# A mixture-of-experts kernel: gathering token rows straight into feature-major tiles

## The chip, the cores and the metric

The kernel runs on one core of a Trainium2 chip. The metric is the device time of one execution in microseconds, as the median of the runs of a kernel.

## The reference, cut to what matters

A decoder trunk of two layers (a gated convolution, then a retention layer), each with cross-attention and a mixture of experts. 288 tokens go through it: 256 of a prompt and 32 of eight short samples. Everything is float32. The part that the change touches is the mixture:

```python
def one_seq(hs):                       # hs: tokens x 1024
    ...                                # top group of 4, then the two best of its 8 experts
    gate = jnp.sum(jax.nn.one_hot(eidx, N_EXPERTS) * wts[..., None], axis=1)
    gu = jnp.einsum('td,edf->tef', hs, w_gate_up)          # 32 experts, 1024 -> 2 x 256
    act = jax.nn.silu(gu[..., :EXPERT_FF]) * gu[..., EXPERT_FF:] * gate[..., None]
    return jnp.einsum('tef,efd->td', act, w_down)          # 256 -> 1024
```

Only two of 32 experts have a nonzero gate for a token, so the kernel computes each expert only for the tokens that chose it.

## The kernel before, in words

The 32 experts of a layer are worked off in 8 **packs** of 4 (`PK`); each expert has 32 slots (`CAP`), so a pack has 128 slots, one per partition. For tokens beyond the slots of an expert there is a second pass (`spill`), a loop whose count is read at run time.

Per pack and layer, `experts(L)` on TensorE does in this order:

- four **gate-up chunks** (`gate_up_chunk`, L905): chunk c multiplies feature tiles 2c and 2c + 1 of `xgT` (features on partitions, slots as columns) by 2 MB of weights; four experts side by side in column tiles of 32. Each waits for its weights to land and its end (`gu_sum`) frees their slot.
- in pack 0 `count_chosen`; then the **gather** `pick(i + 1)` for the next pack. It multiplies a 0/1 matrix `onehot` (tokens x slots, made by `select` on VectorE) with the token rows: `picked_decode` (L872) is four float32 matmuls of 32 rows each for the 32 sample tokens, each on its own quarter of the array's rows, and `picked_prompt(m)` (L879) two full matmuls for the prompt tokens, for each of four blocks of 256 features. The result has slots on partitions, in banks 0, 1, 5 and 6.
- in packs 0, 1, 3 and 5 of layer 0 a projection of the memory for layer 1 (`memory_kv`, L618 and L624), with 2 MB of weights that occupy a slot of the ring;
- the transposes of the gates (L937) and, once ScalarE and VectorE have made them, of the activations (L942); the result of the pack before is spread over the tokens and added (`combine`, L953);
- `turn_x(i + 1)` (L966): ScalarE and VectorE have copied the gathered rows out of the banks to `xg` (`picked_out`, L1539 and L1944); eight transposes (`turn_picked`, L947) turn them, and each engine copies one half to `xgT` (`turned_out`);
- two halves of the down projection (`down_half`, L921); their end (`y_sum`) frees the two slots.

In front of pack 0 stand `pick(0)` and `turn_x(0)`, with nothing in between. A float32 matmul shows in the trace as two instructions, each with its own weight load.

On VectorE (L1958 on) the order is `select(0)`, `gates_known`, `gates(0)`, `picked_out(0)`, `turned_out(0)`, `select(1)`, `passes_known`, and then the packs.

SyncE issues all loads of weights in one fixed order (`RING`). The ring has 7 slots of 2 MB (some loads go to free memory beside it), and each issue waits until the slot's last user is done: in layer 0 the load after that of `dn (0,1,0)` waits for the first memory projection of pack 0, those after it for the two halves of the down projection of pack 0.

Of the kernel before, what the change touches and what calls it, by code (L numbers as in the profile page):

```python
# [23 lines left out]
P = 128  # L24
# [21 lines left out]
SPILL_PE = {"picked": 1, "turned": 2, "gate_up": 3, "gates_turned": 4, "act_turned": 5, "rows": 6}  # L46
SPILL_DVE = {"began": 1, "selected": 2, "gated": 3, "x_out": 7, "xt_out": 9, "gates_out": 10, "silu": 11, "act": 12,
             "actT_out": 13, "rows_out": 15, "added": 23}
STEP_PE, STEP_DVE = 14, 22
# [78 lines left out]
def build(nc, a):  # L128

    with ExitStack() as ctx:  # L130
# [122 lines left out]
        XGO = CATO + 2048 + SLOT  # L253
# [3 lines left out]
        yo, xg = ar(CATO, 1024), ar(CATO + 1024, 1024)  # L257
# [8 lines left out]
        xgT_x, xg_x = v3(ar(HM1, 1024), KD), ar(HM1 + 1024, 1024)  # L266


# [314 lines left out]
        def _(pe):  # L583
# [288 lines left out]
            def picked_decode():  # L872

                for m in range(4):
                    r = slice(32 * m, 32 * m + 32)
                    pe.matmul(bank[X_BANKS[m]][:, 0:256], onehot_m[r, 2, :], htok3[r, :], start=True, stop=False,
                              skip_group_check=True)

            def picked_prompt(m):  # L879

                for b in range(2):
                    mm = pe.matmul(bank[X_BANKS[m]][:, 0:256], onehot_m[:, b, :], htok[b][:, m * 256:(m + 1) * 256],  # L882
                                   start=False, stop=(b == 1), skip_group_check=True)
                return mm
# [60 lines left out]
            def turn_picked(n, src):  # L945
                for k in range(4):
                    mm = pe.transpose(bank[n][:, k * P:(k + 1) * P], src[:, (4 * n + k) * P:(4 * n + k + 1) * P],  # L947
                                      C("ident"))
                return mm

# [4 lines left out]
            def experts(L):  # L955

                def pick(i):
# [45 lines left out]
                pick(0)  # L1003
                turn_x(0)
                for i in range(PACKS):
# [3 lines left out]
                    pe.wait_ge(S("xt_out_a"), PACKS * L + i + 1)  # L1009
                    if i >= 2:  # L1010
                        pe.wait_ge(S("y_added"), KD * PACKS * L + KD * (i - 1))
                    for c in range(4):
                        if c == 2:
                            pe.wait_ge(S("xt_out_d"), PACKS * L + i + 1)
                        if c == 2 and i == PACKS - 1:
                            combine(i - 1, range(0, 5))
                        if c == 3 and i == PACKS - 1:
                            combine(i - 1, range(5, KD))
                        gate_up_chunk(c, gate_up_landed(L, i, c), xgT).then_inc(S("gu_sum"), 1)
                    if i == 0:  # L1020
                        count_chosen()
# [22 lines left out]
                    if i + 1 < PACKS:  # L1044
                        turn_x(i + 1)
# [9 lines left out]
                with pe.If(more > 0):  # L1055
                    pe.wait_ge(S("y_added"), KD * PACKS * L + KD * PACKS)
                    with pe.Fori(0, more) as p:
                        with pe.Fori(0, PACKS) as i:
                            it = p * PACKS + i
                            pe.wait_ge(S(f"spill_dve{L}"), it * STEP_DVE + SPILL_DVE["selected"])  # L1060
                            picked_decode()
                            for m in range(4):
                                mm = picked_prompt(m)
                            mm.then_inc(S(f"spill_pe{L}"), 1)
                            pe.wait_ge(S(f"spill_dve{L}"), it * STEP_DVE + SPILL_DVE["x_out"])
                            turn_picked(0, xg_x)
                            turn_picked(1, xg_x).then_inc(S(f"spill_pe{L}"), 1)
# [1518 lines left out]
```

## Time and profile before

| | |
|---|---|
| three runs | 1156.84, 1157.18, 1157.6 us (median 1157.18) |
| profiled execution: span from first to last instruction | 1157.5 us |
| what lies around the span | not shown apart from the runs' times: the median lies 0.3 us below the span |
| mean granted TensorE clock | 0.98 of full |
| TensorE busy | 1100.7 us, 95% |
| VectorE, ScalarE, GpSimd busy | 510.1, 172.3, 154.0 us |
| read from HBM, written | 339.3, 24.3 MB |

The span starts with layer 0's projections; its experts run from about 287 us to 514 us, the retention layer's mixing from there to 943 us, its experts from 944 us to 1146 us, and the final norm ends the kernel. "Busy" is time in which an engine executes; PE is TensorE's matmuls, PEld its weight loads, which run beside the matmuls. "PEclk" is the share of the full clock (2.4 GHz) that was granted. In the chain of waits each piece is work, or a wait for the engine or transfer that is named, followed back from the last instruction. A DMA piece begins when the slot that it fills was released. The chain's duration of a group is without the overlap with the next; the timeline's includes it, so it is 0.1 to 0.2 us longer.

### The profile page before, as it was taken

To read this page: it belongs to the slowest core of one execution; us is meant where nothing else is said; L and a number is where in the kernel's file an instruction comes from. 1 tells how busy PE (TensorE), PEld (TensorE's weight loads), DVE (VectorE), ACT (ScalarE), POOL (GpSimd) and SP (SyncE) were. 2 spreads that over 40 slices of the span, in tenths; PEclk is the share of its full clock that TensorE was granted. 3 is DMA by queue.
4 is the path that set the end of the run, shared out by engine and by line. 5 is a ranking of instruction groups with operands and counts; after the bars stand their busy time and mean duration, and the time that the engine had idled before them with its cause. 6 is when DMAs were issued, how large, how long until landed. Compare 5 with 4: busy or idle time off the path is not lost.

```text
span 1157.5 us, 17239 instructions
## 1 busy us (share of the span) xinstructions
PE 1100.7 (95%) x7334; PEld 750.3 (65%) x7334; DVE 510.1 (44%) x1089; ACT 172.3 (15%) x410; POOL 154.0 (13%) x103
## 2 busy tenths in 40 slices
PE   8999999999999999979999999999999999987885
PEld 6589997987574545435767657576699755433342
DVE  5446665633213232345444545545465333322234
ACT  2001113013101111020201112020200131100002
POOL 0000001510000000002432324340055100000000
PEclk9999999998999999989999999999999989999998
DMA  9973339835999999969436656487997369999993
GB/s 362 429 273 146 147 146 392 344 146 219 369 429 424 427 426 427 426 270 399 192 154 255 272 208 256 186 332 291 409 422 304 144 270 430 424 427 429 426 427 149
DMA packets 29904, 364.81 MB, mean 315 GB/s; under 512 B 3472, under 2 KB 3616, under 8 KB 7296
## 3 DMA queue, kind: packets, MB, share of 16 engines
q1 hardware_dynamic: 26928, 339.86, 71.4%
q10 hardware_dynamic: 1712, 19.17, 4.0%
q0 software_dynamic: 1184, 4.63, 1.0%
q8 instruction: 61, 1.00, 0.3%
q14 instruction: 19, 0.16, 0.0%
HBM read 339.32 MB, written 24.32 MB: 314 GB/s over the span
## 4 chain that ended last, share of the span: by engine, by line
PE 85%; DMA 13%; DVE 1%; issue 1%; ACT 0%; SPq 0%; DVEq 0%
DMA ring<-in_gu 10%; PE bank L1198 10%; PE bank L725 10%; PE bank L1134 9%; PE bank L910 7%; PE bank L1272 5%; PE bank L624 5%; PE bank L618 4%; PE bank L921 4%; PE bank L882 4%; PE bank L953 3%; DMA ring<-in_dn 3%; PE bank L766 3%; PE bank L1107 3%; PE bank L1191 2%; PE bank L683 1%
## 5 line engine op out<-in xcount | busy, mean ns | idle before, releaser
L910 PE MATMUL bank<-ring,arena 128*32 128x512 f32 x888 | 107.5, 619 | 27.3 <-DMA ring<-in_gu 27.3
L725 PE MATMUL bank<-arena,ring 128*128 128x144 f32 x896 | 110.4, 286 | 1.3 <-issue 1.3
L725 PEld LDWEIGHTS bank<-arena,ring 128*128 128x128 f32 x896 | 110.0, 190 | 1.5 <-issue 1.5
L910 PEld LDWEIGHTS bank<-ring,arena 128*32 128x32 f32 x888 | 28.0, 112 | 97.0 <-issue 67.8
L1933 DVE TENSOR_TENSOR xT<-xT,bank 128x288 f32<-128x288 f32 x128 | 58.2, 455 | 39.2 <-PE bank L953 35.6
L953 PE MATMUL bank<-arena 128*128 128x288 f32 x256 | 70.2, 417 | 3.2 <-issue 2.8
L953 PEld LDWEIGHTS bank<-arena 128*128 128x128 f32 x256 | 46.5, 192 | 27.3 <-issue 11.2
L1198 PEld LDWEIGHTS bank<-ring 128*128 128x128 f32 x448 | 56.2, 190 | 6.0 <-issue 6.0
L882 PE MATMUL bank<-arena 128*128 128x256 f32 x256 | 60.0, 388 | 0.0
L2400 POOL TENSOR_TENSOR ring<-ring 128x1024 f32<-128x1024 f32 x8 | 18.9, 2359 | 307.1 <-DVE arena L2260 307.1
L1198 PE MATMUL bank<-ring 128*128 128x144 f32 x448 | 58.2, 287 | 0.0
L1272 PE MATMUL bank<-ring,hT 128*128 128x512 f32 x128 | 57.2, 597 | 0.0
L921 PE MATMUL bank<-ring,arena 128*32 128x512 f32 x448 | 54.3, 623 | 1.7 <-DMA ring<-in_dn 1.2
L624 PE MATMUL bank<-ring,arena 128*128 128x512 f32 x128 | 55.4, 592 | 0.0
L1927 DVE SCALAR_TENSOR_TENSOR arena<-arena,bank 128x256 f32<-128x256 f32 x16 | 6.7, 419 | 110.4 <-ACT arena L1556 110.4
L882 PEld LDWEIGHTS bank<-arena 128*128 128x128 f32 x256 | 47.7, 191 | 11.5 <-issue 5.6
L2065 DVE SCALAR_TENSOR_TENSOR ring<-ring,bank 128x512 f32<-128x512 f32 x64 | 39.7, 683 | 32.9 <-PE bank L1191 32.9
L618 PE MATMUL bank<-arena,ring 128*128 128x256 f32 x224 | 51.6, 392 | 0.0
L1198 PEld LDWEIGHTS bank<-hT,ring 128*128 128x128 f32 x384 | 48.3, 190 | 2.7 <-issue 2.7
L1198 PE MATMUL bank<-hT,ring 128*128 128x144 f32 x384 | 49.8, 286 | 0.0
L618 PEld LDWEIGHTS bank<-arena,ring 128*128 128x128 f32 x224 | 44.0, 197 | 6.7 <-issue 0.4
L1272 PEld LDWEIGHTS bank<-ring,hT 128*128 128x128 f32 x128 | 23.6, 190 | 30.5 <-issue 30.4
(329 smaller groups left out, 1589.6 us busy)
## 6 DMA issues: line engine op xcount, KB each, us to landing
ring<-in_gu SPq DMA_DIRECT2D x55, 2048.0 KB, 21.6
ring<-in_dn SPq DMA_DIRECT2D x28, 2048.0 KB, 20.2
ring<-in_rin SPq DMA_DIRECT2D x14, 2048.0 KB, 13.4
ring<-in_cin SPq DMA_DIRECT2D x8, 2048.0 KB, 27.3
ring<-in_kc SPq DMA_DIRECT2D x8, 2048.0 KB, 10.1
ring<-in_vc SPq DMA_DIRECT2D x8, 2048.0 KB, 9.5
ring<-in_st SPq DMA_DIRECT2D x8, 2048.0 KB, 8.2
out_rs<-ring ACTq DMA_DIRECT2D x8, 2048.0 KB, 7.1
```

Source lines behind the costliest of these rows:

```text
L618: mm = pe.matmul(bank[KV_BANKS[i][j]][:, o * NM:(o + 1) * NM], w[:, k, f:f + P], src[:, k, :], start=(k == 0), stop=(k == KD - 1), skip_gr ...
L624: mm = pe.matmul(bank[KV_BANKS[i][j]][:, :], src[:, k, mb * P:(mb + 1) * P], w[:, k, :], start=(k == 0), stop=(k == KD - 1))
L725: mm = pe.matmul(out[:, o, :], w[:, o, k, :], x[:, k, :], start=(first and o == 0 and k == 0), stop=(k == 3), skip_group_check=True)
L882: mm = pe.matmul(bank[X_BANKS[m]][:, 0:256], onehot_m[:, b, :], htok[b][:, m * 256:(m + 1) * 256], start=False, stop=(b == 1), skip_group_ ...
L910: mm = pe.matmul(bank[2][32 * e:32 * e + 32, :], xt[:, k, 32 * e:32 * e + 32], w[2 * e + kk], start=(k == 0), stop=(k == KD - 1), skip_gro ...
L921: mm = pe.matmul(out if n == 0 else v3(out, 2), actT[:, f, 32 * e:32 * e + 32], wv[2 * e + f] if n == 0 else wv[:, 2 * e + f], start=(f == ...
L953: return pe.matmul(bank[b][:, 0:T], yo[:, o * P:(o + 1) * P], GT, start=True, stop=True)
L1134: mm = pe.matmul(out[:, o, :], w[:, o, k, :], x[:, k, :], start=(first and o == 0 and k == 0), stop=(k == 3), skip_group_check=True)
L1198: mm = pe.matmul(out[:, o, :], w[o][:, k, :], x[:, k, :], start=(first and o == 0 and k == 0), stop=(k == 3), skip_group_check=True)
L1272: mm = pe.matmul(bank[4 + b][:, :], hT[:, k, b * P:(b + 1) * P], w[:, k, :], start=(k == 0), stop=(k == KD - 1))
L1933: return dve.tensor_tensor(xT[:, o, :], xT[:, o, :], bank[b][:, 0:T], ALU.add)
L2065: dve.scalar_tensor_tensor(out=st[:, j, dt, :], in0=st[:, j, dt, :], scalar=float(np.exp(NS * LOGG[h])), in1=quad_banks(h)[j][:, :], op0=A ...
```

## The change

The gather's operands change places. The token rows (128 features of them) become the stationary operand and `onehot` the moving one, so that the bank holds features on partitions and slots as columns, which is what `xgT` needs. For each of the 8 feature tiles there is one matmul of 32 rows for the sample tokens and two full ones for the prompt tokens, all with 128 columns. `xg`, `turn_picked`, `turn_x` and `turned_out` go; the copies out of the banks write `xgT` directly. In pack 0 the gather of feature tiles 0 to 3 stands in front, tiles 4 and 5 are gathered after gate-up chunk 0, tiles 6 and 7 after chunk 1. On VectorE `picked_out(0)` moves in front of `gates_known` and `gates(0)`. The loop for the second pass is changed in the same way and left out here.

```diff
-            def picked_decode():
-
-                for m in range(4):
+            def picked(m):
+
+                for k in (2 * m, 2 * m + 1):
+                    out = bank[X_BANKS[m]][:, (k % 2) * P:(k % 2 + 1) * P]
                     r = slice(32 * m, 32 * m + 32)
-                    pe.matmul(bank[X_BANKS[m]][:, 0:256], onehot_m[r, 2, :], htok3[r, :], start=True, stop=False,
+                    pe.matmul(out, htok3[r, (k % 2) * P:(k % 2 + 1) * P], onehot_m[r, 2, :], start=True, stop=False,
                               skip_group_check=True)
-
-            def picked_prompt(m):
-
-                for b in range(2):
-                    mm = pe.matmul(bank[X_BANKS[m]][:, 0:256], onehot_m[:, b, :], htok[b][:, m * 256:(m + 1) * 256],
-                                   start=False, stop=(b == 1), skip_group_check=True)
+                    for b in range(2):
+                        mm = pe.matmul(out, htok[b][:, k * P:(k + 1) * P], onehot_m[:, b, :], start=False,
+                                       stop=(b == 1), skip_group_check=True)
                 return mm
...
-                def pick(i):
+                def pick(i, pairs=range(4)):
                     pe.wait_ge(S("selected"), PACKS * L + i + 1)
...
-                    picked_decode()
-                    for m in range(4):
-                        picked_prompt(m).then_inc(S("x_picked"), 1)
-
-                def turn_x(i):
-                    for n in range(2):
-                        pe.wait_ge(S("xg_out_a"), 2 * PACKS * L + 2 * i + n + 1)
-                        pe.wait_ge(S("xg_out_d"), 2 * PACKS * L + 2 * i + n + 1)
-                        turn_picked(n, xg).then_inc(S("xg_turned"), 1)
+                    for m in pairs:
+                        picked(m).then_inc(S("x_picked"), 1)
...
-                pick(0)
-                turn_x(0)
+                pick(0, (0, 1))
                 for i in range(PACKS):
...
-                    pe.wait_ge(S("xt_out_a"), PACKS * L + i + 1)
...
                     for c in range(4):
-                        if c == 2:
-                            pe.wait_ge(S("xt_out_d"), PACKS * L + i + 1)
+                        pe.wait_ge(S("xt_out_d" if c % 2 else "xt_out_a"), 2 * PACKS * L + 2 * i + c // 2 + 1)
                         if c == 2 and i == PACKS - 1:
+                            pe.wait_ge(S("xt_out_d"), 2 * PACKS * L + 2 * i + 2)
                             combine(i - 1, range(0, 5))
...
                         gate_up_chunk(c, gate_up_landed(L, i, c), xgT).then_inc(S("gu_sum"), 1)
+                        if i == 0 and c < 2:
+                            pick(0, (c + 2,))
...
                     if i + 1 < PACKS:
-                        turn_x(i + 1)
+                        pe.wait_ge(S("xt_out_a"), 2 * PACKS * L + 2 * i + 4)
+                        pe.wait_ge(S("xt_out_d"), 2 * PACKS * L + 2 * i + 4)
                     pe.wait_ge(S("actT_out"), PACKS * L + i + 1)
...
                 def picked_out(i):
                     for m in (0, 2):
                         act.wait_ge(S("x_picked"), 4 * PACKS * L + 4 * i + m + 1)
-                        act.activation(xg[:, m * 256:(m + 1) * 256], bank[X_BANKS[m]][:, 0:256], ACT.Copy) \
-                           .then_inc(S("xg_out_a"), 1)
...
+                        act.activation(xgT[:, 2 * m:2 * m + 2, :], picked_bank(m), ACT.Copy) \
+                           .then_inc(S("xt_out_a"), 1)
...
                 select(0)
+                maxima_known(L)
+                picked_out(0)
                 gates_known(L)
                 gates(0)
-                picked_out(0)
-                turned_out(0)
                 dve.wait_ge(S("gated"), PACKS * L + 1)
                 select(1)
```

`maxima_known` is the first part of the old `gates_known` (two small instructions), split off so that ScalarE's exponentials don't wait for the copies. VectorE's `picked_out` and the second pass change alike.

## Rows read from the trace of the kernel before

**Rows 1.** the page: TensorE's busy time, then transfers in 40 slices of the span.
```profile
PE 1100.7 (95%) x7334; PEld 750.3 (65%) x7334; DVE 510.1 (44%) x1089; ACT 172.3 (15%) x410; POOL 154.0 (13%) x103
...
DMA  9973339835999999969436656487997369999993
GB/s 362 429 273 146 147 146 392 344 146 219 369 429 424 427 426 427 426 270 399 192 154 255 272 208 256 186 332 291 409 422 304 144 270 430 424 427 429 426 427 149
```

**Rows 2.** chain that ended last, 285:345: start us, us, what.
```profile
286.83 0.64 PE bank L876 x8
287.47 3.67 PE bank L882 x16
...
291.73 0.63 PE bank L947 x4
292.36 7.00 PE bank L910 x64
...
312.09 0.87 PE bank L947 x8
...
327.69 13.83 PE bank L618 x64
```

**Rows 3.** TensorE's waits, 430:515: us in total, times, longest us.
```profile
PE bank L910 <- DMA ring<-in_gu: 5.8, 4, 2.0
```

**Rows 4.** stretches: us, busy PE to POOL (x instructions), PEclk, DMA share, GB/s.
```profile
294.00:296.00 2.00, 2.00 (x24) 0.65 (x20) 0.00 (x0) 0.00 (x0) 0.00 (x0) 1.00 0.67 193
310.00:313.00 3.00, 3.00 (x24) 2.42 (x26) 0.42 (x1) 1.34 (x3) 0.00 (x0) 1.00 0.48 153
```

**Rows 5.** DMA issues in 311:311.7, 404.5:405, 965.9:966.6, 986.6:987: KB, us to landing.
```profile
ring<-in_dn SPq DMA_DIRECT2D x1, 2048.0 KB, 7.9
...
ring<-in_dn SPq DMA_DIRECT2D x1, 2048.0 KB, 9.0
...
ring<-in_gu SPq DMA_DIRECT2D x1, 2048.0 KB, 9.5
...
ring<-in_gu SPq DMA_DIRECT2D x1, 2048.0 KB, 13.4
```

**Rows 6.** whole chain that ended last: mid-layer rows, and layer 0's memory projection.
```profile
382.96 13.75 PE bank L624 x32
...
779.81 2.16 PE bank L1198 x16
781.97 1.07 PE bank L1191 x8
...
840.82 68.97 PE bank L725 x560
```

**Rows 7.** TensorE's timeline at 323.9:324.1, then line L882: min/median/max ns.
```profile
323.97 0.48 PE L882 MATMUL bank<-arena 128*128 128x256 f32 x1
...
L882 PE MATMUL bank<-arena x256: 379/379/796, 287.4 to 1104.4; 128*128 128x256 f32 x128
```

**Rows 8.** VectorE's timeline, 286.9:289.9: start us, us, line, operation.
```profile
286.93 0.18 DVE L1895 RECIPROCAL arena<-arena 128x3 f32<-128x3 f32 x1 [2.35 <-ACT arena L1534]
...
289.24 0.56 DVE L1922 TENSOR_TENSOR arena<-arena 128x384 f32<-128x384 f32 x1
```

**Rows 9.** half clock: one stretch, then rows of the chain in both layers.
```profile
498.00:506.00 8.00, 6.88 (x37) 1.77 (x37) 1.27 (x3) 0.80 (x2) 0.00 (x0) 0.57 1.00 426
...
498.07 2.70 PE bank L910 x16
...
503.34 3.18 PE bank L921 x16
...
509.48 1.85 PE bank L921 x16
...
1066.86 31.66 DMA ring<-in_gu
...
1134.08 3.54 PE bank L921 x16
```

More of the change, by code:

```diff
@@ L45 @@
 PACKS = NE // PK
[L46 to L49, printed above, removed]
+SPILL_PE = {"picked": 1, "gate_up": 2, "gates_turned": 3, "act_turned": 4, "rows": 5}
+SPILL_DVE = {"began": 1, "selected": 2, "gated": 3, "xt_out": 7, "gates_out": 8, "silu": 9, "act": 10,
+             "actT_out": 11, "rows_out": 13, "added": 21}
+STEP_PE, STEP_DVE = 13, 20
 FIRST = ((0, 2), (2, 4), (4, 8))
@@ L251, in build @@
         assert ro[0] <= PHO + ROUTE and PHO + ROUTE + 3072 <= 20992
-        XGO = CATO + 2048 + SLOT
+        XGO = CATO + 1024
         htok_ = v3(ar(PHO + ROUTE, 2048), 2)
@@ L256, in build @@
         htok3 = ar(PHO + ROUTE + 2048, 256)
-        yo, xg = ar(CATO, 1024), ar(CATO + 1024, 1024)
+        yo = ar(CATO, 1024)
         onehot = ar(SQO, 3 * P).rearrange("p (b c s) -> p b c s", b=3, c=PK)
@@ L264, in build, with picked_bank @@
         xgT = v3(ar(XGO, 1024), KD)
-        xgT_x, xg_x = v3(ar(HM1, 1024), KD), ar(HM1 + 1024, 1024)
+        xgT_x = v3(ar(HM1, 1024), KD)
+        def picked_bank(m):
+            return v3(bank[X_BANKS[m]][:, 0:256], 2)
         def slot(s):
@@ L943, in turn_act @@
                 return mm
[L945 to L949, printed above, removed]
             def spread(o, b):
@@ L1060, in experts @@
                             pe.wait_ge(S(f"spill_dve{L}"), it * STEP_DVE + SPILL_DVE["selected"])
-                            picked_decode()
                             for m in range(4):
-                                mm = picked_prompt(m)
+                                mm = picked(m)
                             mm.then_inc(S(f"spill_pe{L}"), 1)
-                            pe.wait_ge(S(f"spill_dve{L}"), it * STEP_DVE + SPILL_DVE["x_out"])
-                            turn_picked(0, xg_x)
-                            turn_picked(1, xg_x).then_inc(S(f"spill_pe{L}"), 1)
                             pe.wait_ge(S(f"spill_dve{L}"), it * STEP_DVE + SPILL_DVE["xt_out"])
@@ L1541, in picked_out @@
                         act.wait_ge(S("x_picked"), 4 * PACKS * L + 4 * i + m + 1)
-                        act.activation(xg[:, m * 256:(m + 1) * 256], bank[X_BANKS[m]][:, 0:256], ACT.Copy) \
-                           .then_inc(S("xg_out_a"), 1)
-                def turned_out(i):
-                    act.wait_ge(S("xg_turned"), 2 * PACKS * L + 2 * i + 1)
-                    act.activation(xgT[:, 0:4, :], v3(bank[0][:, :], 4), ACT.Copy).then_inc(S("xt_out_a"), 1)
+                        act.activation(xgT[:, 2 * m:2 * m + 2, :], picked_bank(m), ACT.Copy) \
+                           .then_inc(S("xt_out_a"), 1)
                 picked_out(0)
-                turned_out(0)
                 for i in range(PACKS):
@@ L1885, in route, with maxima_known @@
                                             op0=ALU.add, op1=ALU.mult))
-            def gates_known(i):
+            def maxima_known(i):
                 dve.wait_ge(S("rstd_tok"), i + 1)
@@ L1893, in gates_known @@
                    .then_inc(S("gate_maxima"), 1)
+            def gates_known(i):
                 dve.wait_ge(S("gate_exps"), 6 * i + 6)
@@ L1946, in picked_out @@
                         dve.wait_ge(S("x_picked"), 4 * PACKS * L + 4 * i + m + 1)
-                        dve.tensor_copy(xg[:, m * 256:(m + 1) * 256], bank[X_BANKS[m]][:, 0:256]).then_inc(S("xg_out_d"), 1)
-                def turned_out(i):
-                    dve.wait_ge(S("xg_turned"), 2 * PACKS * L + 2 * i + 2)
-                    dve.tensor_copy(xgT[:, 4:8, :], v3(bank[1][:, :], 4)).then_inc(S("xt_out_d"), 1)
+                        dve.tensor_copy(xgT[:, 2 * m:2 * m + 2, :], picked_bank(m)).then_inc(S("xt_out_d"), 1)
                 def add_pack(i, part=range(KD)):
@@ L1980, in experts @@
                     if i + 1 < PACKS:
-                        turned_out(i + 1)
                         dve.wait_ge(S("gt_turned"), PACKS * L + i + 1)
@@ L2015, in experts @@
                             for m in range(4):
-                                dve.tensor_copy(xg_x[:, m * 256:(m + 1) * 256], bank[X_BANKS[m]][:, 0:256]) \
-                                   .then_inc(S(f"spill_dve{L}"), 1)
-                            dve.wait_ge(S(f"spill_pe{L}"), it * STEP_PE + SPILL_PE["turned"])
-                            for n in range(2):
-                                dve.tensor_copy(xgT_x[:, 4 * n:4 * n + 4, :], v3(bank[n][:, :], 4)) \
+                                dve.tensor_copy(xgT_x[:, 2 * m:2 * m + 2, :], picked_bank(m)) \
                                    .then_inc(S(f"spill_dve{L}"), 1)
```

3 lines of the change are left out of this document (removed).

## The prediction

> **What bounds the kernel now.** I read the page first [rows 1]. TensorE is busy for 95% of the span, so time added to it has little slack to vanish in. The two stretches that the change touches are the experts of layer 0 (about 287 to 514 us) and of layer 1 (about 944 to 1146 us). There the transfers run at their full rate too, so each part of these stretches has to be asked which of the two ends last.
>
> The chain of waits for layer 0 [rows 2] shows TensorE pieces without a break through pack 0: gather, transposes, gate-up chunks, the projection of the memory, the transposes of gates and activations. TensorE's list of waits for that stretch has 5.8 us for gate-up weights, in four pieces, all after 430 us [rows 3]. Layer 0 is thus TensorE-bound for its first five packs and shared in the last three. In the page's DMA row the slices from 318 us to 492 us are full [rows 1]. Before that there are two pauses: 294 to 296 us at 193 GB/s and 310 to 313 us at 153 GB/s, against 427 in a full slice [rows 4]. Both end with the issue of a load for whose slot SyncE had to wait. The one of 311 us landed 7.9 us later, which is what a load takes that finds the queue empty; one that finds a queue lands later, at 4.9 us per load (2.10 MB at 427 GB/s) [rows 1, 5]. So a load issued at time t lands at t + 8 or 4.9 us after the one before, whichever is later. The loads issued at 405, 966 and 987 us landed 9.0, 9.5 and 13.4 us later [rows 5]: they had 1.0, 1.5 and 5.4 us to spare before the queue would have run dry. In layer 1 the queue never runs dry, and its last packs go at the pace of the transfers.
>
> **The gather, old and new.** Now one gather takes 0.64 + 3.67 = 4.31 us [rows 2]: 8 instructions of 32 rows (four at a time, side by side) and 16 of the full array (a float32 matmul is two instructions), with 256 columns each. It changes tiling twice, into the 32-row tiles and out of them. The new gather has for each of 8 feature tiles one 32-row matmul and two full ones, with 128 columns: 24 matmuls, 48 instructions. It changes tiling 16 times, and the four 32-row matmuls no longer run side by side.
>
> The bare pace: 560 instructions of 144 columns take 68.97 us, 0.123 us each, so 128 columns take 0.109 us, and transposes with 128 columns take 0.87 / 8 = 0.109 too [rows 2, 6]. 48 x 0.1095 = 5.26 us.
>
> A change of tiling, worked out twice. In the gather, 64 instructions of 256 columns take 13.83 us, 0.216 each; 16 of these and two rounds of the 32-row ones make 18 x 0.216 = 3.89, and 4.31 is 0.42 more, 0.21 per change [rows 2]. In the retention stage 16 full instructions of 144 columns alternate with 8 of 32 rows and 512 columns: 2.16 + 1.07 = 3.23 us, of which 16 x 0.123 + 2 x 0.43 = 2.83 is bare work; 0.40 for two changes, 0.20 each [rows 6]. The timeline shows where it goes: the first full matmul after the 32-row ones takes 0.48 instead of the usual 0.38 us (its weights are loaded in the open, 0.10), and the other 0.10 passes before that load starts [rows 7]. So 16 x 0.20 = 3.2 us, and **a new gather costs 8.46 us**, 4.15 more than the old. Bounds: 5.26 if a change in the middle of an accumulation were free, 9.3 at 0.25 per change. I take 0.20, because both places in the trace give it and the new alternation is of the same two tilings.
>
> **What else is on TensorE.** Removed: the eight transposes, 0.87 us in each of packs 0 to 6 [rows 2], and in front of pack 0 the wait for the row copies and the transposes, 291.14 to 292.36 us, 1.2 us [rows 2]. In pack 0 those 0.87 us also covered the copy of the turned activations on VectorE; without them TensorE waits for it, about 0.45. Added in pack 0: two more returns from the gather to a chunk, 0.4. The copies of rows (4 per pack) become copies into the final tile and the two of 0.6 to 0.7 us go; they hide behind the rest of the gather, so nothing is gained there. VectorE's order changes in pack 0: `gates_known` and `gates`, 286.93 to 289.80 us now, 2.9 us [rows 8], move behind the copy of the last pair, and `select(1)` behind them, for which the second gather waits. The last pair is gathered before chunks 2 and 3, and TensorE has those (3.5 us), a return and `count_chosen` (0.8) to do: 4.5 us against 0.4 + 2.9 + 0.6 = 3.9. It fits, with 0.6 to spare. No DMA issue moves by itself: SyncE's order is the same, and each issue follows TensorE's release of its slot.
>
> **Layer 0.** Eight gathers: 8 x 4.15 = 33.2. Plus 0.4 and 0.45, less 7 x 0.87 = 6.1 and 1.2: TensorE has 26.8 us more to do. Against it stand the waits for transfers, 5.8 [rows 3], which vanish when TensorE is the later one, and the half clock from 499 to 506 us (granted share 0.57 in 498 to 506, one of the two levels, 1.2 GHz) that follows those waits: 3.18 us for 16 instructions that take 1.85 at full clock, and 2.70 for a chunk that takes 7.00 / 4 = 1.75, together 2.3 us [rows 2, 9]. Layer 0 ends 26.8 - 5.8 - 2.3 = **18.7 us later**, if the transfers don't end later still. They: pack 0's early chunk closes the pause at 294 us, but the next load waits for the memory projection behind the second gather, which comes 4.15 + 0.4 - 1.2 + 4.15 = 7.5 us later, so the early slot is given back at once. The load now issued at 405 us follows gathers 0 to 4 and comes 16.9 us later; it has 1.0 to spare, so the transfers fall 16 us behind. TensorE, 26.8 us later before waits are taken off, stays the later one.
>
> **Layer 1.** Its packs go at the pace of the transfers, so only a pause in these counts. The issue at 966 us follows two gathers and the first half of pack 0's down projection: 4.15 + 0.4 - 1.2 + 4.15 - 0.87 + 0.45 = 7.1 us later, with 1.5 to spare: **5.5 us**. The one at 987 us comes 7.1 + 3.3 = 10.4 later with 5.4 to spare, 5.0: no more. From there the reserve is larger than what TensorE loses (3.3 us per pack): it grows with every pack, and by 1067 us a load lands 31.7 us after its slot is released [rows 9].
>
> **Sum.** 1157.5 (span) + 18.7 + 5.5 = 1181.7. The span is 0.3 us above the median of the three times shown, 1157.2; against that median the forecast is **1181 us**.
>
> **The rivals.** *Half of each change is hidden.* The weights of the next matmul are loaded during the last one of the other tiling, and only the 0.10 of emptying is left: gather 5.26 + 1.6 = 6.9 us. Then layer 0 has only 14 us more on TensorE, the transfers are the later ones (8.9 - 1.0 = 7.9), layer 1 loses 3.9 - 1.5 = 2.4: 1167. Against it: the open load in [rows 7]. The Trainium skill ("TensorE: Matmul & The Clock Gate", Step-by-step) says that weight loads are pulled ahead of matmuls in flight when row groups don't conflict or the background buffer is free, which would give this case; "TensorEngine Tiling (Array Packing)", Key Properties, says that a change of tiling mode drains the engine, and gives no price. The rows side with the second.
>
> *A change costs nothing inside an accumulation.* Gather 5.26 us; the issue at 311 us comes 1.1 later, layer 1 loses nothing: 1158, within 0.2%. For it: no row shows a change between two matmuls of one accumulation. Against: the engine, not the bank, changes.
>
> *The clock stays up, and the kernel is faster.* Place: the last packs of both layers, where TensorE idles for transfers and then works at half clock, 2.3 us lost in layer 0 and in layer 1 3.54 instead of 1.8 us for 16 instructions at 1134 us, 1.7 [rows 9]. A longer gather fills that idling. With a gather of 5.26 us this gives 1157.2 + 1.1 - 4.0 = 1154. It decides only if the gather stays under about 5.5 us: each further 0.1 us is paid twice before the load of 311 us, and five times before that of 405 us.
>
> *Dearer than thought.* At 0.25 per change each gather is 0.8 longer, 6.4 us in layer 0 and 1.6 in layer 1: 1189. A missed `selected` in pack 0 adds at most 1.
>
> **Chances.** Forecast (gather 8 to 9 us, 1176 to 1187) 0.78; half hidden 0.08; free 0.06; clock 0.04; dearer than 1189 0.04. The range runs from the half-hidden case to the dearer one, 1165 to 1189, and leaves out about 0.14. A measurement of this kernel can tell 0.2% (2.3 us) from no change: faster 0.04, same 0.05, slower 0.91.
>
> **What would show it.** In the profile after, the gather's line should have 48 instructions per pack in about 8.5 us of the chain, each first weight load after a change starting 0.2 us behind the matmul before. The waits for gate-up weights should be gone from layer 0 and smaller in layer 1, the granted clock full around 518 us, a longer pause of transfers before 319 us and a new one near 992 us. Gathers of 5 to 7 us would prove the forecast wrong, as would layer 0 ending less than 12 us later.

## The result, and the profile after

The changed kernel takes 1190.55 us (four runs: 1184.76, 1186.83, 1194.26, 1197.39) against 1157.39 for the kernel before on the same chip. The ratio is 1.0265, 95% interval 1.0237 to 1.0294: slower, as forecast, but the median lies 1.5 us above the upper end of the range and 9.5 above the forecast. A second set of four runs gave 1186.9 (1185.16 to 1192.14). Each run is 1.7 to 1.9 us longer than its span. The profiled execution is the longest of the first four: 1197.39 us, span 1195.6. One of the 12 runs of the last kernel below took 1409.51 us at a mean granted clock of 0.749 and is left out of the ratio.

The page of the kernel after, rows that answer to [rows 1], with the granted clock and the gather's two lines (L881 the 32 rows of the samples, L884 the prompt), columns as in the page:

```profile
PE 1160.1 (97%) x7590; PEld 796.1 (67%) x7590; DVE 499.1 (42%) x1073; ACT 163.2 (14%) x394; POOL 154.1 (13%) x103
...
PEclk9999999998999999999999999999999959999979
DMA  9964449728699899968436557469995296999992
GB/s 361 428 241 151 170 175 417 283 82 346 276 418 406 354 396 428 427 256 373 197 152 267 243 220 288 196 247 375 428 425 221 88 369 272 425 427 429 425 426 99
...
L884 PE MATMUL bank<-arena 128*128 128x128 f32 x512 | 98.2, 318 | 0.0
...
L881 PE MATMUL bank<-arena 32*128 32x128 f32 x256 | 66.5, 341 | 0.0
```

TensorE went up by 59 us of busy time, and the transfers have new or longer gaps: 276 and 354 GB/s in the slices from 299 and 389 us, and 272 in the one from 986 us, where the same slices of [rows 1] have 369, 427 and 430. The clock's row has a 5 and a 7 in the experts of layer 1 that the kernel before doesn't have.

The chain of waits of after, layer 0, pack 0 (answers to [rows 2]; start us, us, what):

```profile
286.23 0.41 PE bank L881 x2
286.64 0.64 PE bank L884 x4
...
290.45 1.85 PE bank L912 x16
292.30 0.41 PE bank L881 x2
292.71 0.64 PE bank L884 x4
...
302.84 0.30 PE bank L881 x2
303.14 0.64 PE bank L884 x4
...
311.17 6.91 PE bank L622 x32
...
318.88 0.44 DVE arena L1955
```

and its timeline there (start us, us with overlap, shapes):

```profile
303.07 0.71 PE L884 MATMUL bank<-arena 128*128 128x128 f32 x4
303.72 0.48 PE L881 MATMUL bank<-arena 32*128 32x128 f32 x2
304.13 0.71 PE L884 MATMUL bank<-arena 128*128 128x128 f32 x4
```

A feature tile is 0.41 + 0.64 = 1.05 us; the gather for pack 1 begins at 302.7 and the projection behind it at 311.17: 8.45 us. TensorE's waits from 430 to 520 us no longer have a row for gate-up weights (5.8 us before [rows 3]). The only one left is:

```profile
PE bank L944 <- ACT arena L1443: 0.3, 1, 0.3
```

The pause of transfers before the load that was issued at 311 us is longer (answers to [rows 4]; columns as there), and the load lands 8.1 us after its issue at 318.11 [rows 5]:

```profile
312.00:318.00 6.00, 6.00 (x30) 5.23 (x29) 0.00 (x0) 0.00 (x0) 0.00 (x0) 1.00 0.00 0
```

**Where the 38.1 us between the two spans are.** I measure each layer's expert stage from the first instruction of its gather to the end of its last `combine` matmul:

| us | layer 0 | between | layer 1 | span |
|---|---|---|---|---|
| before | 227.6 | 429.7 | 201.5 | 1157.5 |
| after, profiled | 245.9 | 431.5 | 220.0 | 1195.6 |
| after, second profile | 245.9 | 432.4 | 209.5 | 1185.0 |

Layer 0 costs 18.3 us and does so to the hundredth in both profiles; the stretch between, which the change doesn't touch, 1.8 and 2.7; layer 1 costs 18.6 in one and 8.1 in the other. (The start of layer 0 came 0.6 and 1.5 us earlier; with that the sums close.) So layer 1 holds both the error of the forecast and the spread of the runs.

### The profile page after: what moved, and what is told of

The parts are those of the page before. It is cut to its first block, busy times and chain, and to the rows that moved or that the text cites. A ratio compares the mean times of both kernels' runs of the same rounds, so it can differ in the third digit from the quotient of the medians.

```text
span 1195.6 us, 17731 instructions
## 1 busy us (share of the span) xinstructions
PE 1160.1 (97%) x7590; PEld 796.1 (67%) x7590; DVE 499.1 (42%) x1073; ACT 163.2 (14%) x394; POOL 154.1 (13%) x103
## 4 chain that ended last, share of the span: by engine, by line
PE 95%; DMA 3%; DVE 1%; issue 1%; ACT 0%; SPq 0%; DVEq 0%
PE bank L1184 9%; PE bank L729 9%; PE bank L1120 9%; PE bank L912 9%; PE bank L884 7%; PE bank L949 5%; PE bank L1258 5%; PE bank L628 5%; PE bank L881 5%; PE bank L923 4%; PE bank L622 4%; PE bank L1093 3%; PE bank L770 3%; DMA ring<-in_gu 2%; PE bank L1177 1%; PE bank L687 1%
## 5 line engine op out<-in xcount | busy, mean ns | idle before, releaser
L912 PE MATMUL bank<-ring,arena 128*32 128x512 f32 x888 | 106.2, 615 | 5.3 <-DMA ring<-in_gu 5.1
L729 PEld LDWEIGHTS bank<-arena,ring 128*128 128x128 f32 x896 | 110.0, 190 | 1.8 <-issue 1.7
L884 PE MATMUL bank<-arena 128*128 128x128 f32 x512 | 98.2, 318 | 0.0
L884 PEld LDWEIGHTS bank<-arena 128*128 128x128 f32 x512 | 72.4, 204 | 17.0 <-issue 3.4
L1915 DVE TENSOR_TENSOR xT<-xT,bank 128x288 f32<-128x288 f32 x128 | 58.2, 454 | 28.4 <-PE bank L949 24.8
L1929 DVE COPY arena<-bank 128x256 f32<-128x256 f32 x32 | 13.6, 425 | 134.6 <-PE bank L884 134.6
L881 PE MATMUL bank<-arena 32*128 32x128 f32 x256 | 66.5, 341 | 0.0
L949 PEld LDWEIGHTS bank<-arena 128*128 128x128 f32 x256 | 46.7, 192 | 25.3 <-issue 9.2
L881 PEld LDWEIGHTS bank<-arena 32*128 32x128 f32 x256 | 40.5, 197 | 31.9 <-issue 20.2
L923 PE MATMUL bank<-ring,arena 128*32 128x512 f32 x448 | 51.4, 595 | 2.5 <-DVE arena L1955 2.5
## 6 DMA issues: line engine op xcount, KB each, us to landing
ring<-in_cin SPq DMA_DIRECT2D x8, 2048.0 KB, 28.4
```

Of the source, the lines that this page charges most:

```text
L729: mm = pe.matmul(out[:, o, :], w[:, o, k, :], x[:, k, :], start=(first and o == 0 and k == 0), stop=(k == 3), skip_group_check=True)
L881: pe.matmul(out, htok3[r, (k % 2) * P:(k % 2 + 1) * P], onehot_m[r, 2, :], start=True, stop=False, skip_group_check=True)
L884: mm = pe.matmul(out, htok[b][:, k * P:(k + 1) * P], onehot_m[:, b, :], start=False, stop=(b == 1), skip_group_check=True)
L912: mm = pe.matmul(bank[2][32 * e:32 * e + 32, :], xt[:, k, 32 * e:32 * e + 32], w[2 * e + kk], start=(k == 0), stop=(k == KD - 1), skip_gro ...
L923: mm = pe.matmul(out if n == 0 else v3(out, 2), actT[:, f, 32 * e:32 * e + 32], wv[2 * e + f] if n == 0 else wv[:, 2 * e + f], start=(f == ...
L949: return pe.matmul(bank[b][:, 0:T], yo[:, o * P:(o + 1) * P], GT, start=True, stop=True)
```

## The experiments

"Grouped" below means that the 32-row matmuls of several feature tiles are issued together, side by side, and the full ones behind them; "alternating" is the changed kernel's order. All spans, clocks and stages are from one profile each.

### The changed kernel once more

No edit. It gives the runs on this chip and a second profile.

> The changed kernel, unchanged, once more, so that the time can be set against the stretches at half clock of several executions. Theory A (the gather that changes tiling 16 times keeps TensorE's granted clock low once it is low): the spans differ by 5 us or more between executions, and a lower mean granted clock goes with a longer span, about 1 us of span per 2 us at half clock. Rival B (half clock is caused by idle waits alone, as before): executions agree within 2 us and half clock stretches last 3 to 10 us each.

1186.9 us, ratio 1.0242 (1.0203 to 1.0282); the stages stand in the table above. What differs between the profiles is the clock at the start of layer 1. The stretch at 1.2 GHz (PEclk 0.50; columns as in [rows 4]) in the first profile:

```profile
955.40:982.70 27.30, 27.30 (x113) 14.96 (x113) 4.53 (x27) 6.53 (x20) 0.88 (x1) 0.50 0.93 376
```

and in this one:

```profile
953.80:974.30 20.50, 20.37 (x88) 12.25 (x88) 4.59 (x28) 6.28 (x20) 0.87 (x1) 0.50 0.99 393
```

In the kernel before the same place is at half clock for 10.2 us. TensorE's records show it busy for 27.30 of 27.30 and 20.37 of 20.50 us in these stretches, and still the clock stays low.

### Grouped, and grouped in pairs

The first issues the 32-row matmuls of all feature tiles of a call first: two changes of tiling per gather. The second does so for two tiles at a time: eight changes. In both, the second start flag in a bank discards what the 32-row matmul before it had put there, so for every second feature tile the sample tokens' part is missing; the instructions and their sizes are all there. (A version further down discards nothing and is no slower.)

```diff
-                    for m in pairs:
-                        picked(m).then_inc(S("x_picked"), 1)
+                    picked_decode(pairs)       # all 32-row matmuls, four row groups at a time
+                    for m in pairs:
+                        picked_prompt(m).then_inc(S("x_picked"), 1)
```

> Same orientation and same number of matmuls, but the 32-row matmuls of a gather stand together in front of the full ones: 2 changes of tiling per gather instead of 16. If the changes are what costs: a gather takes 16 x 0.22 + 4 x 0.11 + 2 x 0.2 = 4.35 us instead of 8.46, layer 0 and layer 1 lose nothing but the split of pack 0's gather (3 groups, 0.9 us), and the kernel is at 1157 to 1158 us. If the price lies in the orientation (loads of 128-column weights for only 128 columns of work), a gather stays above 7 us and the kernel above 1170.

> The two 32-row matmuls of each pair of feature tiles stand together: 8 changes of tiling per gather. If each change costs 0.20 us: gather 5.26 + 1.6 = 6.9 us, transfers 8 us behind in layer 0 and 2.4 in layer 1: 1167 us, plus what half clock adds. If a change is free, as the changed kernel.

The chain of waits of the grouped kernel, the gather for pack 1:

```profile
299.24 0.53 PE bank L881 x13
299.76 3.77 PE bank L889 x32
```

The same of the kernel with pairs, the first two of four:

```profile
300.16 0.53 PE bank L881 x4
300.69 1.09 PE bank L886 x8
301.78 0.64 PE bank L881 x4
302.41 1.09 PE bank L886 x8
```

The gathers take 4.3, 6.8 and 8.45 us with 2, 8 and 16 changes. The same 32 full instructions take 3.77 us behind one change, and 4.36 and 5.12 us (4 x 1.09, 8 x 0.64) in four and eight pieces: 0.2 us for each entry into the full tiling. Two 32-row instructions take 0.41 us in the alternating order, where two bare ones are 0.22: as much again on the way back. So of the 4.15 us between the first and the last of these gathers 14 changes are 2.8, and the rest is that the grouped order runs the 32-row instructions four at a time. Grouped: 1162.13 us, ratio 1.0017 (1.0001 to 1.0033), layer 0 at 226.6. In pairs: 1172.79, 1.011 (1.0075 to 1.0145), layer 0 at 237.0. So the alternation is the loss, all but 0.2%, and the version with the grouped gather in front, below, has none of that left either: the operands' exchange itself costs nothing in the sum. The second run is also the world of the "half hidden" rival, with its gather of 6.9 us: layer 0 is 9.4 longer, where the rival gave 7.9, and the whole 12.9 longer, where it gave 10.

### Only the first gather of layer 1 grouped

```diff
+                    if L == 1 and i == 0:
+                        picked_decode(pairs)
                     for m in pairs:
-                        picked(m).then_inc(S("x_picked"), 1)
+                        (picked_prompt if L == 1 and i == 0 else picked)(m).then_inc(S("x_picked"), 1)
```

Here too the samples' part is missing for every second feature tile, in that one gather.

> The changed kernel, but the first gather of layer 1 alone (its three parts in pack 0) has its 32-row matmuls grouped. By its work it saves 4.15 - 0.9 = 3.3 us in pack 0. Theory A (alternating gathers keep the clock low): the half clock at the start of layer 1's experts, 27 us in the profile of the changed kernel, gets shorter, to 10 to 17 us, and the load of the third pack's third chunk is issued 8 us or more earlier. Rival B (the wait before the experts sets the clock): 27 us as before and 3.3 us earlier.

The profile has 6.8 us of half clock at that place, less than the 10 to 17 expected, and the stage takes 202.9. But this execution says nothing for theory A. The clock was full again before the gather began, at 963.9 us, so the order of its matmuls can't have ended the half clock:

```profile
954.90:961.70 6.80, 6.47 (x36) 4.55 (x36) 3.16 (x21) 3.29 (x7) 0.88 (x1) 0.50 0.94 360
961.70:963.90 2.20, 1.86 (x16) 0.94 (x15) 1.22 (x6) 0.51 (x2) 0.00 (x0) 0.99 1.00 425
```

So with the same work ahead the half clock lasts 6.8 us in one execution and is still there when the gather begins in others. And the runs are wide, 1180.54 to 1197.25, ratio 1.0257 (1.0197 to 1.0318): the median is that of the changed kernel. The profiled execution was the fastest of the four, and the one of 1197.25 has a mean clock of 0.968. That grouping the first gather alone takes the spread away is not what they show.

### Grouped, all of it in front of pack 0

The grouped order with one start flag per bank, so that nothing is discarded, and without the split of the first gather.

```diff
+                                  onehot_m[r, 2, :], start=(kk == 0), stop=False, ...)
...
-                pick(0, (0, 1))
+                pick(0)
...
-                        if i == 0 and c < 2:
-                            pick(0, (c + 2,))
```

> 32-row matmuls of a gather together in front (as in e1_grouped, here with their accumulation intact), and the first gather of each layer whole in front of pack 0, not in three parts. If the three parts cost 0.9 us for their extra changes and returns 0.4: the load of 311 us is issued 1.1 us earlier than in the kernel before, layer 0 ends 1 us earlier, layer 1 loses nothing: 0.1% faster than before, against 0.2% slower for e1_grouped. If alternating helps (an early slot for the first load), it is slower than e1_grouped.

1158.29 us in 12 runs, ratio 0.9986 (0.9968 to 1.0003), layer 0 at 227.55, layer 1 at 199.5: the kernel before, within what can be told. It has no row copies and no transposes, some 7 us less of TensorE work per layer, and gains nothing, because the transfers end layer 0 then. TensorE's waits from 285 to 520 us:

```profile
PE bank L917 <- DMA ring<-in_gu: 9.3, 6, 3.0
```

That is 3.5 more than before [rows 3]. The work that went is waited for at the end. The last load that the stage uses lands only 1.4 us earlier than before (219.7 us from the stage's start against 221.1), and the last pack gives that back: eight matmul instructions of its `combine` run at half clock and take 4.18 us in the timeline instead of 2.18. The Trainium skill ("PSUM — Partial Sum Buffer", The four PSUM rules) says that two accumulation groups open at once in the same bank and quadrant cannot both begin with the start flag, since the second clears what the first one marked. The two versions of the grouped gather agree: with two flags per bank the samples' part is lost, with one it is kept.

### Alternating, all of it in front of pack 0

The last two hunks of that diff alone.

> The changed kernel with its 16 changes per gather, but the first gather of each layer whole in front of pack 0. By the work alone 0.4 us less per layer and the load after chunk 0 three us later, which the next pause swallows: within 1 us of the changed kernel at the same mean granted clock. If the alternation with chunks is what keeps or loses the clock, the half clock at layer 1's start changes from the 7 to 27 us seen so far.

1187.47 us, 1.0236 (1.0208 to 1.0264); layer 0 at 245.6, layer 1 at 213.2 in the profile. The split of the first gather is worth 0.3 us in layer 0, in the wrong direction, and nothing that the runs could show. The half clock at layer 1's start lasts 27.3 us here too.

### Alternating in layer 0 alone, and everywhere but in the first two gathers of layer 1

Both with one start flag per bank in the grouped gathers.

```diff
+                    alone = L == 1                  # the second kernel: L == 1 and i <= 1
+                    if alone:
+                        picked_decode(pairs)
```

> Alternating gathers in layer 0 only, grouped ones in layer 1: layer 0's share alone. By the forecast 18.7 us over the kernel before (1.6%), with the half clock at layer 1's start back at 10 to 14 us. If layer 1's gathers cost more than 5.5 us, it shows as the difference from the changed kernel (27 us over).

> Grouped gathers in layer 1 for its first two only (the gathers ahead of the load of 966 us), alternating ones elsewhere. If layer 1 loses only through that pause, as forecast, it costs what e6_layer0 costs: 1.6% over before. If the later gathers cost too, because half clock doubles the one that it meets, it lies 3 to 8 us above e6_layer0 in the executions with the lower mean clock.

Layer 0 alone: 1181.27 us (1180.05 to 1181.95), ratio 1.0183 (1.0156 to 1.0211), where 1.6% was expected. In its profile layer 0 costs 18.3 us, the stretch between 2.7 and layer 1, at 203.5, 2.0. The four runs lie within 1.9 us. The half clock at layer 1's start lasts 13.7 us:

```profile
955.80:969.50 13.70, 13.70 (x74) 9.64 (x77) 4.09 (x26) 6.14 (x19) 0.88 (x1) 0.50 0.94 378
```

All but the first two gathers of layer 1: 1181.1 (1177.59 to 1188.33), 1.0168 (1.0139 to 1.0196), layer 1 at 209.5 in the profiled execution, which is the slowest of the five. It is 7.1 us above the median of layer 0 alone, as expected for an execution at a low mean clock (0.976). There the long stretch of low clock is in pack 6, and the start of layer 1 has 13.7 us of it. The stretch in pack 6:

```profile
1123.90:1144.40 20.50, 20.50 (x70) 14.09 (x63) 2.57 (x6) 1.15 (x3) 0.00 (x0) 0.50 1.00 425
```

and the chain of waits in it:

```profile
1123.20 3.02 PE bank L929 x16
1126.22 0.72 PE bank L881 x2
1126.95 1.15 PE bank L884 x4
```

The gather begins behind a wait for weights, at 1.2 GHz, takes 0.72 + 1.15 = 1.87 us per feature tile instead of 1.05, and stays there to its end. So there are two places where an alternating gather can meet a low clock: the start of layer 1, in both profiles of the changed kernel and in the one with the gather in front, and pack 6, in some. Grouping the gathers of one place leaves the other. The kernel with pairs has it in pack 6 too: half clock from 1111.2 to 1128.3 us, 17.1 us, over a gather with eight changes.

### More TensorE work ahead of layer 1

```diff
-                    for _ in range(FILL):
+                    for _ in range(FILL + 3):
```

> The changed kernel with three more filler matmuls of 512 columns on TensorE ahead of the experts of layer 1 (route(1)); nothing computed changes. They cost 2.6 us at full clock and 5.1 us at half. Theory A (the alternating gather keeps a low clock low, but does not lower a high one): the half clock that starts before the first gather of layer 1 ends during the fillers or early in the gather, lasts 14 us or less, the gathers of pack 0 take 8.5 us, the experts of layer 1 take 203 to 207 us, and the whole is level with the changed kernel or up to 5 us faster. Rival (the gather lowers the clock by itself, or what lies before it does and lasts regardless): half clock of 20 us or more at that place as before, the stage of layer 1 at 209 us or more, the whole 3 to 6 us slower than the changed kernel's repeat.

The half clock begins at 956.7 us, about where it does in the other alternating kernels (953.8 to 956.7), lasts 6.8 us and ends during the fillers, at 963.5; the gather begins at 967.3. Stretches of this kernel, around the fillers and in the gather:

```profile
956.00:968.00 12.00, 11.66 (x58) 6.47 (x58) 4.10 (x26) 4.11 (x10) 0.88 (x1) 0.72 0.96 377
968.00:978.00 10.00, 10.00 (x70) 5.68 (x70) 0.43 (x1) 2.31 (x12) 0.00 (x0) 1.00 1.03 423
```

The alternating gather does not lower a full clock: 1.00 through it. Layer 1 takes 205.0 us instead of 209.5 and 220.0. The fillers cost 2.3 of it back (the stretch between is 434.7), and the whole is level with the changed kernel: 1185.72 (1183.69 to 1192.35), ratio 1.023 (1.0202 to 1.0259), against 1.0242; the upper part of the hoped-for gain did not come. The rival that the gather lowers the clock by itself falls. That the fillers ended the half clock is not shown, since it lasted 6.8 us without them too (only the first gather grouped), and one of the four runs here took 1192.35 us at a mean clock of 0.982.

### The memory projection ahead of the second gather

In pack 0 of layer 0, on TensorE and for its copy on ScalarE, once in the grouped version and once in the changed kernel. `count_chosen` moves in both layers.

```diff
+                        if i == 0 and c == 3:
+                            count_chosen()
                         gate_up_chunk(c, ...)
...
-                    if i + 1 < PACKS:
-                        pick(i + 1)
-                    if i == 0:
+                    if L == 0 and i == 0:
                         (the memory projection)
+                    if i + 1 < PACKS:
+                        pick(i + 1)
```

> Grouped gather, all of it in front of pack 0 (the version that came out level with the kernel before), and in pack 0 of layer 0 the memory projection and its copy now stand ahead of the second gather, with count_chosen moved between chunks 2 and 3 so that VectorE's copies still find it. The load now released by that projection (issued at 311 us in the kernel before, at about 307 in the grouped one) is released one grouped gather, 4.3 us, earlier. Theory (the two pauses of transfers in pack 0 of layer 0 are a bound of this version, since its transfers end layer 0): the second pause shrinks from 3.3 us to nearly nothing and the expert stage of layer 0 takes 224.5 us (224 to 225.5) instead of 227.6; the whole is 0.2 to 0.4% faster than the kernel before. Rival (the later releases, after the down projection of pack 0, are the bound, as they keep their place): the stage stays at 227 to 228 us and the time is the same within 0.2%.

> The changed kernel (alternating gather) with the same move: memory projection of pack 0, layer 0, ahead of the second gather. Theory (TensorE alone bounds layer 0 in the changed kernel): the load issued at 318 us comes 8.4 us earlier, at about 310, the pause of transfers before it goes, and the stage still takes 245.9 us, within 0.5. Rival (the longer pause is what lengthens layer 0): the stage becomes 3 us shorter or more, 243 us or less. Span 1180 to 1190 us, depending on layer 1, which is unchanged.

*In the changed kernel* the load is issued at 310.8 instead of 318.1 us, 8.0 earlier counted from the start of the stage, and layer 0 takes 246.4 us: 0.5 more. With alternation TensorE alone ends layer 0. Its one run took 1192.68 us, with a span of 1190.9, just above the 1180 to 1190 expected; the half clock at layer 1's start lasted 27.3 us in it, and layer 1 took 214.1.

*Grouped:* layer 0 takes 224.1 us, as the theory said, and the whole 1155.4 us in six runs, ratio 0.9974 (0.9951 to 0.9997). But the last load that the stage uses lands only 0.6 us earlier than in the version without the move (219.1 against 219.7 us from the start), since part of the pause comes back one load later, which lands 6.3 us behind the one before instead of 4.9. The rest is the clock of the last pack. At 502 to 508 us, grouped without the move:

```profile
502.00:508.00 6.00, 5.26 (x22) 2.54 (x15) 0.91 (x2) 2.64 (x5) 0.00 (x0) 0.53 0.97 415
```

and with it:

```profile
502.00:508.00 6.00, 4.55 (x32) 1.86 (x24) 2.44 (x5) 3.73 (x7) 0.00 (x0) 1.00 0.88 377
```

Was that luck? The same kernel again:

> The grouped version with the memory projection first, unchanged, once more. Its first profile had the stage of layer 0 at 224.1 us, 3.5 shorter than the grouped version without the move, but its transfers ended only 0.6 us earlier; the other version had 6.8 us of half clock in the last pack, this one none there. Theory (the clock stayed up because the last pack's waits are shorter and fewer, so it does so each time): no half clock between 495 and 515 us again, stage 224.1 us within 0.5, time 0.1 to 0.4% below the kernel before. Rival (the clock was luck, and only the transfers' 0.6 us are the move's own): half clock of 6.8 us near 500 us, stage 226 to 227 us, and a time within 0.1% of the kernel before.

Stretches of its profile, the second pause of transfers and the last pack:

```profile
308.00:312.00 4.00, 3.28 (x31) 2.85 (x33) 1.70 (x4) 0.88 (x3) 0.00 (x0) 1.00 1.00 426
502.00:508.00 6.00, 4.49 (x30) 1.85 (x24) 2.51 (x5) 3.73 (x7) 0.00 (x0) 1.00 0.90 385
```

The pause is closed (426 GB/s; 238 in the grouped version without the move), the clock is full again, layer 0 takes 224.0, ratio 0.9977 (0.9963 to 0.9992). It recurs, and this version is 0.25% faster than the kernel before, the only one whose interval lies below 1. The interval of the version without the move, 0.9968 to 1.0003, overlaps it, so that the move itself gains is likely and not shown: the 3.5 us of layer 0 are in the profiles, and some 1 us between the ratios. My reason for the clock, shorter and fewer waits, is not borne out: TensorE's waits for gate-up weights after 460 us are 5.2 us without the move, 5.9 and 4.5 with it. Why the clock stays up is open.

## Why the prediction was right in direction and short in size

**The bound, and the gather's price.** Right. 8.46 us was forecast for a gather at full clock, 8.45 measured; 0.20 us per change holds from 2 to 16 changes, also between two matmuls of one accumulation, which no row of before showed. So the free rival (5.26) and the half-hidden one (6.9) fall. The weight loads of after show why: within a tiling a load starts 0.11 us ahead of its matmul (303.18 against 303.29 us), and the first one behind a change starts with it (303.07, 303.71, 304.13 us). The Trainium skill ("TensorE: Matmul & The Clock Gate", Step-by-step) says that weight loads are pulled ahead of matmuls in flight when the row groups don't conflict or the load goes to the background weight buffer. The trace agrees within a tiling, and shows no such load across a change.

**Small terms of pack 0.** The copy of the turned activations leaves TensorE idle from 318.86 to 319.56, 0.70 us, where I said 0.45. The chunks take 1.85 each behind a gather instead of 1.75, as the two returns were meant to. VectorE's order fits: nothing waits for `selected`.

**Layer 0.** Forecast 18.7 us, measured 18.3. The load of 311 us comes 7.35 us later (said: 7.5), the one of 405 us 17.1 (said: 16.9), and its landing falls 15.9 behind (said: 16). The waits for weights are gone, and TensorE ends the stage, as the run with the earlier load shows. The 2.3 us of half clock that I booked as regained were regained in the stage, and most of it was lost right after. The chain of after, behind the last `combine`:

```profile
534.44 0.21 issue
534.65 9.69 PE bank L1093 x32
```

Before, these 32 instructions take 8.00 us at full clock; here 3.4 us of the stretch, from 535.6 us, are at half clock, and that costs 1.7. The stretch between the stages is 1.8 to 2.7 us longer. That is the first failing step: a gain counted within a stage's borders, and the stretch between put at nothing. Whether one half clock brings on the other is open. The two profiles of the grouped kernel with the memory projection first have no half clock from 280 to 931 us, so one can be without both. I said that the granted clock would be full around 518 us; it is, and half at 535.6.

**Layer 1.** Forecast 5.5 us, measured 8.1 and 18.6: the term that was mis-sized. The mechanism is the one forecast, a pause of transfers before the load that was issued at 966 us. Counted from the start of the stage, that load is issued at 22.2 us before, 28.4 with the fillers (6.2 later; I said 7.1), 33.3 in the second profile (11.1 later) and 37.1 in the first (14.9 later). The last landing is 5.2, 9.7 and 13.8 us later than before. Only with the fillers, where the gathers run at full clock, is it near the forecast's 5.5 (and the stage 3.5 longer, since less is left to do behind the last landing). The pause in the profile of after:

```profile
995.00:1001.00 6.00, 5.28 (x43) 3.08 (x45) 1.87 (x4) 1.10 (x3) 0.00 (x0) 1.00 0.01 3
```

The failing step is that I priced this gather at full clock, though it starts at 1.2 GHz. The trace of before had the sign of it: its half clock of 936.0 to 946.2 us reaches 2.2 us into the stage, whose first gather takes 1.17 + 4.16 = 5.33 us instead of 4.31:

```profile
944.13 1.17 PE bank L876 x8
945.29 4.16 PE bank L882 x16
```

I had the cost per change at full clock only; the chain of after gives the other:

```profile
963.62 0.72 PE bank L881 x2
964.34 1.15 PE bank L884 x4
...
971.11 3.57 PE bank L912 x16
```

1.87 us per feature tile, 15.0 per gather, 6.5 more than at full clock. And the half clock lasts longer under it. It overlaps the stage for 2.2 us in the kernel before, 10.8 in the second profile of after and 19.2 in the first. At a loss of 0.44 of the time (1 - 1.055 / 1.87) these last two cost 4.7 and 8.4 us, and the load is 4.9 and 8.7 us later than with the fillers. The accounts meet within 0.3 us.

The remaining 4.8 us of the profiled execution (18.6 - 13.8) come behind the last landing: its stage ends 11.5 us after it, that of the second profile 5.0. The slow stretch is in pack 6. TensorE waits 2.2 and 3.0 us for weights there, falls to half clock at 1132.9, begins the gather so and is slow for 20.5 us:

```profile
1132.90:1153.40 20.50, 20.50 (x70) 14.00 (x63) 2.57 (x6) 1.15 (x3) 0.00 (x0) 0.50 1.01 429
```

In the second profile the half clock lasted 6.8 us (1124.4 to 1131.3) and ended before this gather began (1131.7), and this term is absent. I had written that from 987 us on the reserve of transfers is larger than what TensorE loses. That holds only for gathers at full clock.

**The rival on the clock** was right in layer 0's last packs, which stay at full clock, and had the wrong sign in layer 1's. I let a longer gather fill the idling and keep the clock up. In pack 6 it came behind the wait, when the clock was already low, and the clock stayed there. The start of layer 1 was not among its places.

**The sum.** With layer 1 as in the fillers' run, 18.3 + 2 + 3.5 us would give a span of 1181.3, the forecast's 1181.7. That it meets so closely is partly luck: the 2 us between the stages stood at nothing in my sum, and layer 1's 5.5 was 2 too much for this case. The eight executions of the changed kernel have spans of 1182.9 to 1195.6, and their mean granted clock falls with it from 0.988 to 0.974. The range had no case for that. "0.3 us between span and median" was no measure of what lies around the span either, which is 1.8; it only said that the profiled execution was slow among its fellows.

## What to carry to other kernels

An operation split between two tilings of TensorE should change tiling once, not per tile: here each change cost 0.20 us at full clock, and the order of issue decided between level and 2.4 to 2.6% slower. When adding TensorE work, look up the granted clock at the place where it goes and price it at that level, and follow a clock gain past the end of the stage before booking it. Work removed from a stage that the transfers end came back here as 3.5 us more of waiting at its end; releasing one load 4.0 us earlier moved the last landing by only 0.6.

## What was not expected of the hardware

Half clock under gapless work. In four profiles an alternating gather begins at 1.2 GHz at the start of layer 1: both of the changed kernel, the one with the gather in front and the one with the memory projection first. There the low stretch lasts 27.3, 20.5, 27.3 and 27.3 us, 10.8 to 19.3 of them from the gather's start on. In seven profiles the gather that begins at 1.2 GHz there is the old or a grouped one, and the clock is full again 1.3 to 5.6 us after its start; two of the seven, alternating in layer 0 and grouped here, have the work of the changed kernel ahead of it. In the other three (pairs, only the first gather grouped, fillers) the low stretch of 3.4 to 6.8 us is over before the gather begins, and they can't bear on it. The same gather started at full clock runs at full clock, as the row of the run with fillers shows. That a low clock lasts longer under the alternation than under the grouped order is shown by these profiles, one or two for each kernel; by what, no run tells.
